# The feed-forward gate and up products by Strassen's scheme, in a two-block transformer kernel on one core

## The reference

```python
D_FF = 2816
def swiglu(h, w_gate, w_up, w_down):
    return (jax.nn.silu(h @ w_gate) * (h @ w_up)) @ w_down
...
x_lat = x_lat + m_lat[2][:, None] * rms_norm(y_lat, norm_mix_post[layer])
f_lat = swiglu(modulate(rms_norm(x_lat, norm_ffn_pre[layer]), m_lat[3], m_lat[4]),
               w_gate[layer], w_up[layer], w_down[layer])
x_lat = x_lat + m_lat[5][:, None] * rms_norm(f_lat, norm_ffn_post[layer])
```

## Time and profile before

| | |
|---|---|
| median of 3 runs | 3366.23 us (3365.5 to 3369.23) |
| the profiled execution | 3367.72 us, of which the span is 3365.6 us |
| PE, weight loads, DVE, ACT, POOL busy | 97%, 77%, 51%, 39%, 8% of the span |
| granted clock of PE | 0.985 of full speed over the span |
| the FFN in the trace | from 770 to about 1516 us |

### The profile page before, as it was taken

How to read it: one execution, slowest core, us unless ns; L and a number is a source line. 1 busy time by engine, 2 the same in 40 slices (tenths; PEclk the granted TensorE clock), 3 DMA queues, 4 the chain that set the end, 5 groups by cost and what they waited for, 6 DMA issues and landing times.

```text
span 3365.6 us, 43745 instructions
## 1 busy us (share of the span) xinstructions
PE 3256.9 (97%) x18179; PEld 2586.0 (77%) x18179; DVE 1728.2 (51%) x2425; ACT 1297.3 (39%) x2235; POOL 253.0 (8%) x302
## 2 busy tenths in 40 slices
PE   6899888899999999999999999999999999999999
PEld 6577656787878878889955579999999555688887
DVE  6777576555353444346554553444546545534433
ACT  4432455544232333234345542333333355423322
POOL 1000313500000000000120000000000300000001
PEclk7999989999999999999999999999999999999999
DMA  6445213133333334333200113342432001123323
GB/s 248 158 150 167 85 48 114 52 119 126 116 109 100 95 94 169 94 91 112 102 1 7 51 48 89 124 138 85 143 133 77 14 7 51 47 88 132 109 94 113
DMA packets 97750, 328.24 MB, mean 98 GB/s; under 512 B 11457, under 2 KB 12881, under 8 KB 96785
## 3 DMA queue, kind: packets, MB, share of 16 engines
q1 hardware_dynamic: 77120, 252.55, 23.1%
q0 software_dynamic: 18896, 68.63, 5.9%
q10 hardware_dynamic: 1536, 4.26, 0.3%
HBM read 299.19 MB, written 26.21 MB: 97 GB/s over the span
## 4 chain that ended last, share of the span: by engine, by line
PE 88%; DVE 6%; ACT 2%; DMA 2%; issue 1%; DVEq 0%; POOL 0%; SPq 0%; ACTq 0%; POOLq 0%
PE psum L146 87%; DVE mixer L175 2%; PE psum L149 1%; DVE mixer L185 1%; DVE junk L189 1%; DVE wlo L175 1%; DMA stage<-in_wm 1%; DMA stage<-in_wi 0%; ACT whi L163 0%; ACT mixer L154 0%; DMA hold<-in_wq 0%; ACT arena L154 0%; ACT mixer L155 0%; DVE mixer L194 0%; DVE mixer L180 0%
## 5 line engine op out<-in xcount | busy, mean ns | idle before, releaser
L146 PE MATMUL psum<-region,whi 128*128 128x260 f32 (+2 forms) x7616 | 1831.7, 333 | 1.8 <-DVE region L185 1.8
L146 PEld LDWEIGHTS psum<-region,whi 128*128 128x128 f32 (+1 forms) x7616 | 1279.5, 186 | 164.6 <-DVE region L185 3.1
L146 PE MATMUL psum<-region,wlo 128*128 128x260 f32 (+2 forms) x3808 | 1265.8, 332 | 0.0
L175 DVE TENSOR_TENSOR wlo<-stage,whi 128x1024 fp32r<-128x1024 f32 (+2 forms) x454 | 509.8, 1124 | 611.6 <-ACT whi L163 610.9
L146 PEld LDWEIGHTS psum<-region,wlo 128*128 128x128 f32 (+1 forms) x3808 | 711.2, 187 | 78.6
L163 ACT CAST whi<-stage 128x1024 fp32r<-128x1024 f32 (+2 forms) x454 | 432.6, 968 | 220.6 <-PE psum L146 172.3
L154 ACT ACTIVATE arena<-psum 128x512 f32<-128x512 f32 (+2 forms) x412 | 193.2, 469 | 776.1 <-PE psum L146 772.9
L146 PE MATMUL psum<-arena 128*128 128x512 f32 (+11 forms) x1072 | 382.4, 479 | 1.9 <-ACT arena L154 1.4
L163 ACT COPY arena<-psum 128x260 f32<-128x260 f32 (+9 forms) x345 | 151.7, 444 | 409.8 <-PE psum L146 402.9
L175 DVE TENSOR_TENSOR arena<-arena,psum 128x512 f32<-128x512 f32 (+1 forms) x220 | 125.9, 572 | 329.1 <-PE psum L146 329.0
L175 DVE TENSOR_TENSOR arena<-arena 128x512 f32<-128x512 f32 (+8 forms) x341 | 204.6, 617 | 151.5 <-ACT arena L154 145.1
(11 more groups left out here) (167 smaller groups left out, 2704.4 us busy)
## 6 DMA issues: line engine op xcount, KB each, us to landing
stage<-in_w SPq DMA_DIRECT2D x144, 512.0 KB, 3.5
stage<-in_wi SPq DMA_DIRECT2D x55, 512.0 KB, 4.3
stage<-in_wo SPq DMA_DIRECT2D x48, 512.0 KB, 3.5
stage<-in_wg SPq DMA_DIRECT2D x44, 512.0 KB, 3.5
stage<-in_wu SPq DMA_DIRECT2D x44, 512.0 KB, 3.5
stage<-in_wm SPq DMA_DIRECT2D x42, 512.0 KB, 3.7
stage<-in_wd SPq DMA_DIRECT2D x32, 512.0 KB, 3.5
arena<-xr_scratch POOLq DMA_DIRECT2D x5, 2080.0 KB, 9.6
```

The lines of the kernel that those rows point to most:

```text
L146: return Issued(self, self.e and self.e.matmul(out, w, x, start=start, stop=stop, skip_group_check=True))
L175: return Issued(self, e and e.tensor_tensor(out, a, b, op))
```

## The change

Two k-halves, two halves of 256 tokens and two tiles of 128 hidden columns make a 2x2 by 2x2 product of blocks. It is computed in Winograd's form of Strassen's scheme: seven products in place of eight. `PRODUCTS` names for each product the block or sum of the weights (11, 12, 21, 22, T1 to T4) and of the activations (a11, a12, a22, s1 to s4), and its PSUM bank (a to d). A product has 4 k-tiles x 3 matmuls of 256 columns. Block 12 is only summed, not multiplied (`PART`). M2, M3 and M4 are accumulated on top of M1, M5 and M7 in the same bank, after ACT has copied those to `m1`, `m5`, `m7`.

- The weight sums T1 to T4 are made by POOL (`pool_weights`), each an add of two staged tiles of 128x512, and then split by ACT and DVE like a loaded block.
- Staging and halves are rings of slots of 512 columns (6 and 8); a gate or up pair has 4 loaded blocks of 256 KB and 4 sums, 7 of the 8 are split. The look-ahead of ACT and DVE is a table (`AHEAD`).
- The activation sums s1 to s4 are made by DVE. Class `Quarters` takes the place of `Halves` for `hf`: eight shifts (the bias of the modulation) and then seven casts, four sums and seven low parts of 128x1024.
- The results are combined by DVE, 256 columns at a time: U = M1 + M6, C12 = M3 on M5 minus U, V = U + M7, C21, C22. Silu is applied to C11 from PSUM and to the other three at once; the multiply by up, likewise.
- There are six ticks in each step over a pair of columns (`j`), three in each down unit of part 2 of the first half. `positions` moves to the front of its list, `xload` of ("r", 1) behind the splits of `("in", 0, 0)`, six gaps come ahead of that norm.
- Memory: the buffers of activations, outputs and norms are laid out anew (`nx[1]` in the place of `xc`, one `yd` for both halves). Slots 6 and 7 of staging (`W.more`) are named, but every ring uses six.

```diff
+def quarters(K, c0, c1):
+    h = K // 256
+    return [(k, h, c + d, 128) for c in range(c0, c1, 256) for k, d in ((0, 0), (0, 128), (h, 128), (h, 0))]
...
-    "wg": fm(1024, 0, DFF),
-    "wu": fm(1024, 0, DFF),
+    "wg": quarters(1024, 0, DFF),
+    "wu": quarters(1024, 0, DFF),
...
+    def pair(self, key, name, j, done):
+        us = {}
+        for n, b in enumerate(("11", "12", "22", "21")):
+            if b == "22":
+                us["T1"] = self.take((key, "T1"), name, 4 * j, SUM, done, "unit", self.u, width=1,
+                                     source=(us["11"], us["12"]))
+            if b == "21":
+                us["T3"] = self.take((key, "T3"), name, 4 * j, SUM, done, "unit", self.u, width=1,
+                                     source=(us["12"], us["22"]))
+                us["T2"] = self.take((key, "T2"), name, 4 * j, SUM, done, "unit", self.u, width=1,
+                                     source=(us["T1"], us["22"]))
+            us[b] = self.take((key, b), name, 4 * j + n, PART if b == "12" else SPLIT, done, "unit", self.u, width=1)
+        us["T4"] = self.take((key, "T4"), name, 4 * j, SUM, done, "unit", self.u, width=1, source=(us["T2"], us["21"]))
+        self.pairs[key] = us
+        return us
...
+    def room(self, u):
+        out = [c[s] for c, s in self.first.get(self.spot[u], ())]
+        for v in self.sprev[u]:
+            kind = self.seq[v][2]
+            if kind == RAW:
+                out.append(self.used(v))
+            if kind in (SPLIT, SUM):
+                out.append(self.lo[v])
+            if v in self.reader:
+                out.append(self.summed[self.reader[v]])
+        return out
...
+def pool_weights(e, W, upto):
+    while W.sum_u <= min(upto, len(W.seq) - 1):
+        u = W.sum_u
+        W.sum_u += 1
+        if W.seq[u][2] != SUM:
+            continue
+        for f in W.room(u):
+            e.wait_ge(*f)
+        a, b = W.source[u]
+        e.wait_ge(*W.landed(a))
+        e.wait_ge(*W.landed(b))
+        e.tensor_tensor(W.staged(u), W.staged(a), W.staged(b), ALU.add, own=False).then_inc(*W.summed.up(u))
...
+PRODUCTS = (("M1", "11", "a11", "a"), ("M5", "T1", "s1", "c"), ("M7", "T3", "s3", "d"), ("M6", "T2", "s2", "b"),
+            ("M3", "22", "s4", "c"), ("M2", "21", "a12", "a"), ("M4", "T4", "a22", "d"))
+KEPT = {"M1": "m1", "M5": "m5", "M7": "m7"}
+AHEAD = (5, 7, 9, 10, 11, 12, 12)
+def pe_pair(e, W, bank, psum, key, name, j, h, done, A, leave, tick):
+    us = W.pair(key, name, j, done)
+    begun = {}
+    for n, (p, blk, x, b) in enumerate(PRODUCTS):
+        u = us[blk]
+        if b not in begun:
+            at, free = bank.take((key, b), *leave[b])
+            for f in free:
+                e.wait_ge(*f)
+        else:
+            at = bank.of[key, b]
+            e.wait_ge(*A[key, KEPT[begun[b]]])
+        o = psum[:, at, 0:256]
+        wh, wl = [y.rearrange("p (k n) -> p k n", n=128) for y in W.halves(u)]
+        kt = W.shape(u)[1]
+        e.wait_ge(*h(x))
+        e.wait_ge(*W.hi[u])
+        e.wait_ge(*W.lo[u])
+        for k in range(kt):
+            e.matmul(o, wh[:, k, :], h.hi[x][:, k, :], b not in begun and k == 0, False)
+            e.matmul(o, wh[:, k, :], h.lo[x][:, k, :], False, False)
+            ins = e.matmul(o, wl[:, k, :], h.hi[x][:, k, :], False, k == kt - 1)
+        ins.then_inc(*done.up("unit", u))
+        done.mark(key, p)
+        begun.setdefault(b, p)
+        tick(n)
...
+    ACT_ORDER = ("a11", "a22", "a12", "s1", "s3", None, None, "s2", None, None, "s4")
+    DVE_ORDER = (("lo", "a11"), ("lo", "a22"), ("sum", "s1"), ("sum", "s3"), ("lo", "a12"), ("lo", "s1"), ("sum", "s2"),
+                 ("lo", "s3"), ("lo", "s2"), ("sum", "s4"), ("lo", "s4"))
...
+        self.at = {"a11": a, "a12": b, "a22": d, "s1": d, "s3": c, "s2": a, "s4": b}
+        self.sums = {"s1": (d, c, d, ALU.subtract), "s3": (c, a, c, ALU.subtract), "s2": (a, d, a, ALU.subtract),
+                     "s4": (b, b, a, ALU.add)}
...
+        return [("shift", self, k) for k in range(8)] + [("quarter", self, i) for i in range(11)]
...
+    FFN0 = [("xload", ("x", 1), 0), ("positions", 0, 0)] + n_post[1][1] + n_pre[1].steps() + [("angles", 0, 0)]
+    FFN1 = [("xload", ("r", 0), 0)] + n_end0[1] + 6 * GAP + n_in[0].steps(6, 0, 0)
...
-                act_weights(e, W, W.last[key] + 2)
+                act_weights(e, W, W.last[key] + (8 if (ch, m) == (1, 7) else 2))
...
+    def ahead(key, n, last):
+        return W.pairs[key]["11"] + (min(AHEAD[n], 9) if last else AHEAD[n])
+    def ahead_down(key, m):
+        return W.last[key] + (6 if m >= 6 and key[1:3] != (1, 2) else 2)
...
+        def low_of(j, j0):
+            k = 2 * (j - j0)
+            e.wait_ge(*A["uh", ch, j])
+            e.tensor_tensor(ul[:, k:k + 2], gq[(11 * ch + j) % 2], uh[:, k:k + 2].bitcast(F32), ALU.subtract,
+                            own=False).then_inc(*D.up("ul", ch, j))
...
+                        dve_weights(e, W, ahead(key, n, (name, j) == ("wu", j0 + nj - 1)))
+                        o = psum[:, bank.of[key, b], 0:256]
+                        if p == "M6":
+                            e.wait_ge(*A[key, "m1"])
+                            e.wait_ge(*T[key, p])
+                            e.tensor_tensor(m1, m1, o, ALU.add, own=False).then_inc(*D.up(key, "U"))
+                            if name == "wg" and j > j0:
+                                low_of(j - 1, j0)
+                        if p == "M3":
+                            e.wait_ge(*D[key, "U"])
+                            e.wait_ge(*T[key, p])
+                            e.tensor_tensor(c12, o, m1, ALU.subtract, own=False).then_inc(*D.up(key, "C12"))
+                        if p == "M2" and name == "wu":
+                            e.wait_ge(*A[("wg", ch, j), "C11"])
+                            e.wait_ge(*T[key, p])
+                            e.tensor_tensor(g[:, 0:256], g[:, 0:256], o, ALU.mult, own=False).then_inc(*D.up(key, "C11"))
+                        if p == "M4":
+                            e.wait_ge(*A[key, "m7"])
+                            e.tensor_tensor(m7, m1, m7, ALU.add, own=False).then_inc(*D.up(key, "V"))
+                            e.wait_ge(*T[key, p])
+                            e.tensor_tensor(c21, o, m1, ALU.add, own=False).then_inc(*D.up(key, "C21"))
+                            e.wait_ge(*A[key, "m5"])
+                            e.wait_ge(*D[key, "V"])
+                            e.tensor_tensor(c22, m5, m7, ALU.subtract, own=False).then_inc(*D.up(key, "C22"))
+                            if name == "wu":
+                                e.wait_ge(*A[("wg", ch, j), "silu"])
+                                e.tensor_tensor(g[:, 256:1024], g[:, 256:1024], tu, ALU.mult).then_inc(*D.up("u", ch, j))
...
+    def pool_ffn(e, bs):
+        for ch, todo in enumerate((FFN0, FFN1)):
+            bs.todo += todo
+            pool_weights(e, W, W.pairs["wg", ch, 0]["T4"])
+            bs.tick()
+            pool_weights(e, W, W.pairs["wu", ch, 0]["T4"])
+            for part, (j0, nj) in enumerate(PARTS):
+                for j in range(j0, j0 + nj - 1):
+                    pool_weights(e, W, W.pairs["wu", ch, j + 1]["T4"])
+                    bs.tick(6)
+                bs.tick(12)
+                if part < 2:
+                    pool_weights(e, W, W.pairs["wg", ch, j0 + nj]["T4"])
+                    bs.tick(2)
+                    pool_weights(e, W, W.pairs["wu", ch, j0 + nj]["T4"])
+            bs.flush()
...
-            e.wait_ge(*sffn.dve["lo", ("in", 0, 0), 7])
-            e.wait_ge(*sffn.act["hi", ("in", 0, 0), 7])
+            pool_moves(e, "xload", ("r", 1))
+            e.wait_ge(*sffn.pe["end"])
```

More of the change, by code:

```diff
@@ L248, in take, with __init__, align, place @@
         return b, [c[s] for c, s in free]
+SPLIT, RAW, PART, SUM = range(4)
 class Weights:
     NS, NH = 3, 4
-    def __init__(self, S, H, L, land, hi, lo, aps):
-        self.S, self.H, self.L, self.land, self.hi, self.lo, self.aps = S, H, L, land, hi, lo, aps
-        self.seq, self.half, self.by, self.last, self.count = [], [], {}, {}, 0
-        self.rows = None
+    def __init__(self, S, H, L, land, hi, lo, summed, aps):
+        self.S, self.H, self.L, self.land, self.hi, self.lo, self.summed, self.aps = S, H, L, land, hi, lo, summed, aps
+        self.seq, self.width, self.spot, self.half, self.sprev, self.hprev = [], [], [], [], [], []
+        self.by, self.last, self.pairs, self.source, self.reader, self.first = {}, {}, {}, {}, {}, {}
+        self.rows, self.more = None, None
+        self.align(0, 0, 2 * self.NS)
+        self.sown, self.hown = [None] * (2 * self.NS + 2), [None] * (2 * self.NH)
         self.restart()
     def restart(self):
-        self.u = self.hi_u = self.lo_u = self.sp_u = 0
-    def take(self, key, name, i, raw, count, *step):
+        self.u = self.hi_u = self.lo_u = self.sp_u = self.sum_u = 0
+    def align(self, spot, half, spots):
```

(44 more changed lines are left out.)

290 lines of the change are left out of this document (172 added, 118 removed).

## The result

The changed kernel takes 3438.0 us (median of 4 runs, 3434.8 to 3443.3) against 3367.1 us before (median of 4): a ratio of 1.0216, with a 95% interval of 1.0204 to 1.0228. It is slower, as the forecast of 3376 us said, but by seven times as much, and outside the range of 3330 to 3408. The profiled execution took 3434.8 us, with a span of 3433.0, which is 67.4 us more than the span before.

What follows compares the result with a forecast made beforehand. PE was taken to bound the kernel. From 3366.2 us, -55 (PE) + 50 (stall) + 11.5 (start) + 3 (ends of parts) = +9.5 gave 3376 us, own range 3360 to 3395, with 3330 to 3408 as the wider range.

Steps and rivals of the forecast that it cites:

- PE's gain: FFN gate and up products: 84 matmuls of 256 columns replace 48 of 512 per pair, giving back 55 us, bounds 48 and 62.
- DVE's own work: Gate and up part of four j: DVE needs 55.7 us plus work beside, against 79.6 us of PE.
- The lock: GpSimd's weight sums shut out DVE instructions with two SBUF inputs, 0.9 us each; 22.7 us delay per part of four j.
- The stall that follows from it: Four heavy gate and up parts: about all work beside turns into PE stall, 50 us, bounds 17 and 77.
- Parts with nothing beside: Part 2 of each half, three j: DVE some 57 of 59.7 us, so no stall.
- The start: Start of the FFN: first products wait for ACT's and DVE's splits and the clock drops; +11.5 us, between 8 and 15.
- The ends of the parts: From M4 to u's low part, about 4.2 us only partly covered by the down unit: +3 us, bounds 0 to 6.
- DMA at nothing: Weight loads in half pieces and the moved load of x: same bytes, each load with several us to land, no cost.
- The first (the port hardly costs): Rival: sums fall where DVE waits for PE or reads PSUM; stall 17 us, kernel 3341 us; chance 0.30.
- no overlap, and waits on top: Rival: heavy parts stall 77 us, start 15, ends 6, PE at the 260-column price; kernel 3416 us; chance 0.22.
- a fixed price on short matmuls: Rival: at 0.134 us per 256-column matmul PE gains nothing, and more makes even stages without stalls slower; chance 0.02.
- The signs of being right: Matmuls at 0.118 us, PE waiting for low parts, DVE at 90%, slower subtractions and POOL adds, some 8 us start gap.

Runs made afterwards that it cites:

- experiment 1: Changed kernel with GpSimd's weight sums covering only 16 of their 512 columns (outputs not the reference's): 3355.2 us.
- experiment 4: Changed kernel with the norms' root steps in the FFN taken apart, with gaps between DVE's addition, PE and ACT, and the reciprocal: 3427.3 us.
- experiment 7: Changed kernel with the weight sums made by DVE and the norms' root steps taken apart with gaps: 3391.0 us.
- experiment 3: Changed kernel with the weight sums made by DVE, two units ahead of each low part, instead of GpSimd: 3399.1 us.
- experiment 6: Changed kernel with the norms and adds beside the FFN handed out later, mostly in down parts: 3424.9 us with GpSimd's sums, 3392.7 us with DVE's.
- experiment 9: On experiment 7, part 1 of each chunk freed of beside steps: 3365.6 us; then also eight staging slots and sums four units ahead: 3360.0 us.

## Why the prediction was wrong

- **PE's gain: right.** 60.7 us where the forecast had 55 with bounds 48 and 62. The price at 256 columns is 0.1169 us, a little under the line through 260 and 512.
- **DVE's own work: right.** Without the lock (experiment 1) DVE is busy 79.9, 66.3, 73.8 and 67.8 us in the heavy parts; the forecast had 55.7 and the beside work, 73.0, 67.8, 73.6 and 68.9. The first is 6.9 too low: five steps of 1.14 us of the first pair, which the start's term counts, make 5.7 of it.
- **The lock: right in sum, its pieces off.** Busy DVE time in the four parts is 371.8 us with the sums and 287.8 without, over 110 sums: 0.76 us each, where 22.7 for 29 is 0.78. A sum undisturbed takes 1.26 us and not 1.06, and one that hits in full holds DVE up by 1.1 us and not 0.9, so not every sum hits in full.
- **The stall that follows from it: this is the step that failed.** It said: "I take 50 us, a little above the middle", between 17 and 77. The heavy parts take 421.7 us against 4 x 78.6 = 314.3. Of the 107.4 between, 7 belong to the start, so 100 stand against the 50.

  Experiment 1 splits them. Without the holds the four parts still take 350.0 us: 36 over PE's work, 29 without the start. The forecast had nothing there, since DVE needs 73 us at most ("That alone would fit"), and it said "Without any lock it would be 3324"; the run took 3355.2. The other 71 us come with the sums. So the sums' share was too low, and the stall that is there without them was left out.

  Seen from DVE: its busy time exceeds PE's work by 57.5 us (371.8 - 314.3), near to what its own terms gave (78.4 + 2 and the beside work, less 79.6, in four parts: 63.7). The other 50 us are time in which the late engine is itself idle: 13.9, 10.5, 10.0 and 15.5 us in the four windows. The upper bound, "with no overlap at all", took DVE for busy throughout and so was no bound.

  Two mechanisms are seen behind it. PE's queue holds root matmuls that wait for the end of DVE's backlog, and after each of them ACT and DVE wait for PE (experiments 4 and 7: 8 to 11 us). They are not the whole: in part 1 of the first half, which holds none, DVE is idle for 10.5 us as well. And PE's clock: 36 us of the 42.3 that slow matmuls cost in the FFN lie in these four windows (PE busy 350.4 us for 314.3 of work), where the forecast had 2 us, at the start alone. In experiment 1, with fewer stalls, it is 16 us there. That stalls bring the low clock is read from the rows and not shown by an experiment: in experiment 4 PE's idle time falls and its slow matmuls do not. The rest, DVE's waits for roundings whose sum or load came late, has no price of its own: experiments 3, 6 and 9 each change more than that, and how the 71 us divide stays open.
- **Parts with nothing beside: "no stall" was wrong by 7 us.** They take 62.8 and 62.4 us where 504 matmuls take 58.9, and 58.9 exactly without whole sums.
- **The start: right, with 2 us of the lock in it.** PE, GpSimd and DVE at the start of the FFN, in the timelines of the changed kernel:

```profile
761.79 0.39 PE L151 MATMUL psum<-y_hi,wlo 128*128 128x512 f32 x1
762.02 1.95 PE L151 MATMUL psum<-cst 128*128 128x128 f32 x16
772.94 0.80 PE L151 MATMUL psum<-region,whi 128*128 128x256 f32 x2 [8.97 <-DVE region L180]
...
778.66 0.77 PE L151 MATMUL psum<-region,whi 128*128 128x256 f32 x2 [2.79 <-issue]
...
768.07 3.71 POOL L180 TENSOR_TENSOR stage<-stage 128x512 f32<-128x512 f32 x3
...
769.52 4.50 DVE L180 TENSOR_TENSOR region<-arena,region 128x1024 fp32r<-128x1024 f32 x2 [2.96 <-ACT region L168]
...
776.21 2.35 DVE L180 TENSOR_TENSOR region<-arena,region 128x1024 fp32r<-128x1024 f32 x2
```

The forecast counts from the end of the last matmul of `wo`, here 762.2 us; the 16 matmuls of `cst` behind it are fill, and the 8.97 us count from their end. M1 was to begin at 8.5 us and begins at 10.8. The sums explain it: three of them run from 768.07 to 771.78 us, and DVE's first two low parts take 4.50 us where two later ones take 2.35. In experiments 1 and 3, without GpSimd's whole sums, M1 begins at 8.4 and 8.7. M4 was to end at 24.3, with the clock 26.3; the first pair is done near 790.0, at 27.8. So 18 us are lost where 16.3 were forecast, and against the 4.7 of the kernel before that is +13, within the bounds of 8 and 15. From 778.66 to 783.28 the granted clock is 0.50 (1.2 GHz).
- **The ends of the parts: mis-sized.** Six waits for `region` make 17.8 - 9.0 = 8.8 us, where the forecast had 3 and bounded it by 6.
- **DMA at nothing: right; ACT: off by up to 8.7 us.** ACT's `m` copies held PE for 8.7 us in 7 waits, as part of the same chain. No wait of PE is ended by a load.
- **The rivals.** The first (the port hardly costs) needed under 34 us of stall. The second, "no overlap, and waits on top", came nearest in kind: 3416. Its waits existed, but it priced only those at the starts and ends. The third, a fixed price on short matmuls, is refuted by the 0.1169 us.
- **The signs of being right** came nearly all (waits for `wlo`, DVE busy for 85 to 91% of the heavy parts, subtractions of 958 ns, the gap at the start), and the time was wrong all the same: they would look alike with 50 us of stall and with 100.

## What to carry to other kernels

When an engine that was half idle is loaded up to the length of the engine that sets the pace, its total is no estimate of the stall: here the late engine was itself idle for 50 of 422 us. At 88 us of DVE for 79 of PE the part was 20 us too long, not 9. At 70 for 79, with no root matmul in the part, it was 1 to 4 us too long; at 68 for 79, with one (experiment 1), 9. Before work is given to GpSimd because it is idle, price what its reads take from DVE's instructions with two SBUF inputs: 176 sums that took POOL 0.28 ms beside everything else cost 78 us of the kernel, more than the 61 us for which they were made. And look for matmuls of other work in PE's queue: where one waits for a backlog, PE pays at once what it could have caught up on.

## What was not expected of the hardware

- A tensor_tensor of 128x512 on GpSimd takes 1.26 us at the least and 1.59 on the mean beside DVE: it is held up in its turn (1.76 us at 798.92, where it met an instruction of DVE's under way).
- A memset of GpSimd's of 128x992 two-byte elements (0.92 us) held up none of DVE's 301 subtractions that the mean would show (687 ns); an add of nearly the same length holds one up by 1.1 us.
- An adding DMA of 256 KB from SBUF to SBUF, issued by GpSimd, lands in 4.1 us (median of 176) where a load of 256 KB from HBM takes 3.1 beside it, and 2.6 without such transfers.
- After PE's waits of 8.97 us (until 772.94) and 9.57 us (until 1213.37) matmuls of 256 columns come at 0.21 us instead of 0.12, at a granted clock of 0.50. Over the 112 us of part 0, in which PE is busy for 91.5, the granted clock is 0.89.
